# Two transformer blocks on one Trainium2 core: first MLP layer in two-tile units with merged matmuls, and a new order of small work at two norms

## The reference, cut to what matters

```python
        x = x + g1 * (mixed @ w_out[l])
        h2 = rms_norm(x) * (1.0 + sc2) + sh2
        x = x + g2 * (jnp.square(jax.nn.relu(h2 @ w_ff1[l])) @ w_ff2[l])
    return rms_norm(x, final_norm_w)
```

## Time and profile before

| what | value |
|---|---|
| time, median of 3 executions | 947.14 us (946.02 to 947.41) |
| the profiled execution | 945.35 us |
| its span, first to last instruction | 943.6 us |
| mean granted clock of PE | 0.989 of full |
| PE busy | 929.3 us, 98% |
| DVE busy | 708.4 us, 75% |
| ACT busy | 544.4 us, 58% |
| POOL busy | 118.6 us, 13% |
| moved by DMA | 175.47 MB, mean 186 GB/s |
| ff1 on PE | 428.2 to 520.8 us of the span |
| ff2 on PE | 520.8 to 610.6 us |
| in2's first group on PE | 610.6 to 626.7 us |

### The profile page before, as it was taken

How to read it: one execution, slowest core, us unless ns; L and a number is a source line. 1 busy time by engine, 2 the same in 40 slices (tenths; PEclk the granted TensorE clock), 3 DMA queues, 4 the chain that set the end, 5 groups by cost and what they waited for, 6 DMA issues and landing times.

```text
span 943.6 us, 17987 instructions
## 1 busy us (share of the span) xinstructions
PE 929.3 (98%) x6932; PEld 864.8 (92%) x6932; DVE 708.4 (75%) x934; ACT 544.4 (58%) x746; POOL 118.6 (13%) x95
## 2 busy tenths in 40 slices
PE   8999999999999999999999999999999999999997
PEld 5799999999899889989999888899878999999886
DVE  5947788889999968567666546679976698877664
ACT  4366655666676665455555435557675676666542
POOL 0000200035655400010000001302200100000000
PEclk8999999999999999999999999999999999999999
DMA  9954555577767756544566665535333356655661
GB/s 334 355 186 134 169 189 180 180 227 242 229 216 246 242 177 217 183 156 136 178 180 187 202 187 185 156 131 169 126 130 112 113 178 187 195 183 189 191 213 49
DMA packets 74952, 175.47 MB, mean 186 GB/s; under 512 B 5440, under 2 KB 32464, under 8 KB 74896
## 3 DMA queue, kind: packets, MB, share of 16 engines
q1 hardware_dynamic: 73920, 172.39, 56.5%
q0 software_dynamic: 368, 1.31, 0.4%
q10 hardware_dynamic: 608, 1.00, 0.3%
HBM read 173.63 MB, written 1.05 MB: 185 GB/s over the span
## 4 chain that ended last, share of the span: by engine, by line
PE 83%; DVE 11%; issue 3%; DMA 2%; ACT 1%; DVEq 0%; SPq 0%; ACTq 0%
PE proj_ps L1601 18%; PE proj_ps L1602 17%; PE proj_ps L1603 17%; PE proj_ps L1618 11%; PE proj_ps L1621 6%; DVE w_lo L925 4%; DVE mod_acc L937 3%; PE proj_ps L1661 1%; PE proj_ps L1662 1%; PE proj_ps L1663 1%; PE aux L1970 1%; PE aux L1689 1%; DMA mod_first<-in_panels 1%; PE aux L1697 1%; PE aux L1997 1%
## 5 line engine op out<-in xcount | busy, mean ns | idle before, releaser
L925 DVE TENSOR_TENSOR w_lo<-raw,w_hi 128x1024 fp32r<-128x1024 f32 x276 | 350.3, 1287 | 148.1 <-ACT w_hi L468 147.6
L468 ACT CAST w_hi<-raw 128x1024 fp32r<-128x1024 f32 x276 | 286.6, 1047 | 217.3 <-PE proj_ps L1603 101.5
L1601 PE MATMUL proj_ps<-act_pair,w_hi 128*128 128x256 f32 x1248 | 356.0, 285 | 0.0
L1603 PE MATMUL proj_ps<-act_pair,w_lo 128*128 128x256 f32 x1248 | 353.0, 283 | 0.0
L1602 PE MATMUL proj_ps<-act_pair,w_hi 128*128 128x256 f32 x1248 | 353.0, 283 | 0.0
L1601 PEld LDWEIGHTS proj_ps<-act_pair,w_hi 128*128 128x128 f32 x1248 | 239.2, 192 | 4.0 <-issue 2.5
L1602 PEld LDWEIGHTS proj_ps<-act_pair,w_hi 128*128 128x128 f32 x1248 | 239.3, 192 | 0.9 <-issue 0.2
L1603 PEld LDWEIGHTS proj_ps<-act_pair,w_lo 128*128 128x128 f32 x1248 | 239.3, 192 | 0.0
L1618 PE MATMUL proj_ps<-ff_pair,w_hi 128*128 128x512 f32 x256 | 69.9, 394 | 0.0
L432 POOL TENSOR_TENSOR tmp_b<-tmp_b 128x512 f32<-128x512 f32 x4 | 5.2, 1295 | 467.2 <-ACT tmp_b L491 467.2
L1618 PE MATMUL proj_ps<-glu_pair,w_hi 128*128 128x512 f32 x176 | 50.0, 395 | 0.0
(11 more groups left out here) (333 smaller groups left out, 1528.7 us busy)
## 6 DMA issues: line engine op xcount, KB each, us to landing
raw<-in_panels SPq DMA_DIRECT2D x308, 512.0 KB, 4.3
mod_first<-in_panels SPq DMA_DIRECT2D x16, 512.0 KB, 11.1
xres<-in_x_t SPq DMA_DIRECT2D x2, 512.0 KB, 6.3
out_t<-tmp_a SPq DMA_DIRECT2D x4, 256.0 KB, 2.1
wst<-in_ws_t POOLq DMA_DIRECT2D x1, 512.0 KB, 3.9
bs_sb<-in_bs_rows POOLq DMA_DIRECT2D x1, 512.0 KB, 4.9
level_sb<-in_levels ACTq DMA_DIRECT2D x1, 512.0 KB, 4.6
cols<-in_cols SPq DMA_DIRECT2D x1, 267.0 KB, 2.9
```

The source lines that it names most:

```text
L468: nc.scalar.copy(w_hi[:, s, :], raw[:, s, :]).then_inc(hi_done, 1)
L925: tt(out=w_lo[:, s, :], in0=raw[:, s, :], in1=w_hi[:, s, :].bitcast(F32), op=ALU.subtract).then_inc(taken, 1)
L1601: mm(dst, hi, xh, start=first and k == 0 and nt % 2 == 0, stop=False, skip_group_check=True)
L1603: ins = mm(dst, lo, xh, start=False, stop=last and k == ks - 1, skip_group_check=True)
```

## The change

ff1's group 1 stays a chunk, now in half 1 of `proj_ps`. Groups 2 to 8 become 14 units of two tiles, two slots each, run by `unit_panel` and loaded by `load_unit`. Since a bank now holds two halves, ACT copies the second half of a unit's two banks to `half_sb`, DVE adds the first half to it (`ffsum_sb`), and takes max(s, 0) * s in one operation (`ffsq_sb`), which is relu and square; ACT copies the high part and DVE subtracts for the low part. PE's wait for a free half becomes a wait for the square. The loops of ff1 are written out. At the norm in front of ff1 the residuals of tiles 6 and 7 go ahead of `split_lo` of slots 0 and 1, and `split_lo` of slot 2 moves into the norm, behind tile 3. In in2 the column sums come one tile at a time behind the first three half panels, and `row_of` behind the fifth.

```diff
-EVAC_XBC, EVAC_ZG, EVAC_FF1, EVAC_IN2, EVAC_UP = 4, 12, 20, 27, 33
+EVAC_XBC, EVAC_ZG, EVAC_FF1, EVAC_IN2, EVAC_UP = 4, 12, 20, 34, 40
...
-            with sp.Fori(out_rg + 2, ff2) as i:
+            for s in range(SLOTS):
+                load(out_rg + 2, s)
+            for rg in range(out_rg + 3, ff2):
                 for s in range(SLOTS):
-                    load(i, s)
+                    load_unit(rg, s, rg, s // 2, s % 2)
...
-            for s in range(2):
-                split_hi(GROUP["ff1"], s)
+            split_hi(GROUP["ff1"], 0)
             squares((6,), RES_OUT)
+            split_hi(GROUP["ff1"], 1)
             split_hi(GROUP["ff1"], 2)
             squares((7,), RES_OUT)
...
+            split_all(GROUP["ff1"] + 1)
+            evac(relu_sb[:, 0].rearrange("p (n t) -> p n t", n=NT), GROUP["ff1"], 1, ACT.Relu)
+            act.wait_ge(S["sq_ok"], 1)
+            nc.scalar.copy(ff_hi[:, 0:NT], sq_sb[:, 0].rearrange("p (n t) -> p n t", n=NT)).then_inc(S["ffhi_ok"], 1)
+
+            def small_half(u):
+
+                act.wait_ge(used, (GROUP["ff1"] + 1) * SLOTS + 2 * u + 2)
+                nc.scalar.copy(half_sb[:, u % 2], proj_ps[:, u % 2].rearrange("p (n a t) -> p n a t", n=2, a=2)[:, :, 1]
+                               ).then_inc(evac_act, 1)
+
+            def ff_high(u):
+                act.wait_ge(S["sq_ok"], u + 2)
+                nc.scalar.copy(ff_hi[:, 2 * u + 4:2 * u + 6], ffsq_sb[:, u % 2]).then_inc(S["ffhi_ok"], 1)
+
+            for c in range(1, 8):
+                for h in range(2):
+                    split_hi(GROUP["ff1"] + c + 1, 2 * h)
+                    small_half(2 * c - 2 + h)
+                    split_hi(GROUP["ff1"] + c + 1, 2 * h + 1)
+                    ff_high(2 * c - 2 + h)
...
             add_unit(1, (4, 5), 16)
-            split_lo(GROUP["ff1"], 0)
             dve.wait_ge(S["bank_done"], 1)
             add_unit(0, (6,), 16)
-            split_lo(GROUP["ff1"], 1)
+            split_lo(GROUP["ff1"], 0)
             dve.wait_ge(used, (GROUP["out"] + 2) * SLOTS)
             add_unit(0, (7,), 16)
-            split_lo(GROUP["ff1"], 2)
+            split_lo(GROUP["ff1"], 1)
...
+            norm_apply(1, lambda k: modc[:, 32 + k:33 + k], lambda k: modc[:, 24 + k:25 + k],
+                       lambda k: split_lo(GROUP["ff1"], {3: 2, 7: 3}[k]) if k in (3, 7) else None)
...
+            def ff_square(u):
+
+                dve.wait_ge(evac_act, EVAC_FF1 + u + 2)
+                step(tt(out=ffsum_sb[:, u % 2], in0=half_sb[:, u % 2],
+                        in1=proj_ps[:, u % 2].rearrange("p (n a t) -> p n a t", n=2, a=2)[:, :, 0], op=ALU.add))
+                stt(out=ffsq_sb[:, u % 2], in0=ffsum_sb[:, u % 2], scalar=0.0, in1=ffsum_sb[:, u % 2], op0=ALU.max,
+                    op1=ALU.mult).then_inc(S["sq_ok"], 1)
...
+            def ff_low(u):
+                dve.wait_ge(S["ffhi_ok"], u + 2)
...
+            for c in range(1, 8):
+                for h in range(2):
+                    split_lo(GROUP["ff1"] + c + 1, 2 * h)
+                    ff_square(2 * c - 2 + h)
+                    split_lo(GROUP["ff1"] + c + 1, 2 * h + 1)
+                    ff_low(2 * c - 2 + h)
...
+            chunk(GROUP["ff1"], 1, x_ready=(S["nrm_lo"], KT))
+            for u in range(14):
+                if u == 1:
+                    pe.wait_ge(evac_act, EVAC_FF1 + 1)
+                elif u > 1:
+                    pe.wait_ge(S["sq_ok"], u)
+                for kk in range(2):
+                    unit_panel(GROUP["ff1"] + 1 + u // 2, 2 * (u % 2) + kk, u % 2, act_hi, act_pair, kk, 4, kk == 0)
             for u in range(4):
                 if u < 2:
-                    pe.wait_ge(evac_act, EVAC_FF1 + 7 + u)
+                    pe.wait_ge(S["sq_ok"], 14 + u)
...
-                    pe.wait_ge(S["ff_ok"], 2 * (kk // 2) + 2)
+                    pe.wait_ge(S["ff_ok"], 4 * (kk // 2) + 3)
...
             def beside_in2(s, half):
+                if (s, half) == (0, 0):
+                    mean_square(2, (0,), True)
                 if (s, half) == (0, 1):
-                    mean_square(2, (0, 6, 7), True)
-                if (s, half) == (1, 1):
+                    mean_square(2, (6,), True)
+                if (s, half) == (1, 0):
+                    mean_square(2, (7,), True)
+                if (s, half) == (2, 0):
                     row_of(2)
```

More of the change, by code:

```diff
@@ L160, in two_blocks @@
         ff_hi, ff_lo = ff_pair[:, :, 0], ff_pair[:, :, 1]
-        relu_sb = at("relu_sb", 136, [2, NT * T])
-        sq_sb = at("sq_sb", 144, [2, NT * T])
+        relu_sb = at("relu_sb", 136, [1, NT * T])
+        sq_sb = at("sq_sb", 144, [1, NT * T])
+        half_sb = at("half_sb", 148, [2, 2, T])
+        ffsum_sb = at("ffsum_sb", 152, [2, 2, T])
+        ffsq_sb = at("ffsq_sb", 156, [2, 2, T])
         q_sb = at("q_sb", 72, [4, T])
@@ L1265, in _ @@
             broadcast(1, stat[:, 1])
[L1266 to L1275, removed]
@@ L1277, in _ @@
-            with dve.Fori(0, 4) as i:
-                ff1_step(i * 2, 0)
-                ff1_step(i * 2 + 1, 1)
+            norm_apply(1, lambda k: modc[:, 32 + k:33 + k], lambda k: modc[:, 24 + k:25 + k],
+                       lambda k: split_lo(GROUP["ff1"], {3: 2, 7: 3}[k]) if k in (3, 7) else None)
+            split_all(GROUP["ff1"] + 1)
+            dve.wait_ge(evac_act, EVAC_FF1 + 1)
+            tt(out=sq_sb[:, 0], in0=relu_sb[:, 0], in1=relu_sb[:, 0], op=ALU.mult).then_inc(S["sq_ok"], 1)
@@ new lines, in _ @@
+            dve.wait_ge(S["ffhi_ok"], 1)
+            tt(out=ff_lo[:, 0:NT], in0=sq_sb[:, 0].rearrange("p (n t) -> p n t", n=NT), in1=ff_hi[:, 0:NT].bitcast(F32),
+               op=ALU.subtract).then_inc(S["ff_ok"], 1)
+            def ff_square(u):
[4 more added lines that the diff above has]
+                    op1=ALU.mult).then_inc(S["sq_ok"], 1)
@@ new lines, in ff_low @@
+            def ff_low(u):
+                dve.wait_ge(S["ffhi_ok"], u + 2)
+                part = slice(2 * u + 4, 2 * u + 6)
+                tt(out=ff_lo[:, part], in0=ffsq_sb[:, u % 2], in1=ff_hi[:, part].bitcast(F32), op=ALU.subtract).then_inc(S["ff_ok"], 1)
+            for c in range(1, 8):
[4 more added lines that the diff above has]
+                    ff_low(2 * c - 2 + h)
```

## The result

| | before | after |
|---|---|---|
| median of 4 executions each, us | 947.12 (946.02 to 947.41) | 939.51 (938.80 to 941.84) |
| ratio, 95% interval | | 0.9926 (0.9907 to 0.9945) |
| the profiled execution, us | 945.35 | 941.84 |
| its span, us | 943.6 | 940.1 |
| mean granted clock | 0.989 | 0.993 |

7.6 us faster, 5.2 to 8.8 by the interval. The direction was right, the size was not.

A forecast was written before the change was run, and what follows sets the result against it. PE was taken as the bound, busy for 98% of the span. Gains of 2.06 + 1.1 + 0.4 = 3.6 us gave 943.5 us against the median of 947.14, chance 0.50, range 941.0 to 946.3.

The forecast's parts named there:

- Part 1: ff1: two-tile units with merged matmuls bring 28 slots from 2.880 to 2.807 us each, gaining 2.06 us on PE.
- rival C: ff1: DVE becomes the bound, at ff_square behind w_lo; at most 6 us slower, about 950 us; chance 0.07.
- Rival D: ff1: merging matmuls saves nothing, the 2.06 us falls away and 1.5 is left, 945.6 us; chance 0.03.
- Part 2: Norm before ff1: residuals ahead of w_lo start sum, root, row_of and norm earlier; 1.1 us taken, ends 0 and 1.8.
- case for the clock that stays up: Norm before ff1: without the low clock row_of is short and the chunk starts near 426.5; gain 1.8 us.
- the case of 0.5: Norm before ff1: the low clock comes at the same moment again, keep_clock ends near 427.6; gain 0.5 us.
- Part 3: in2: column sums over three half panels avoid the low clock; 0.4 us taken, ends -0.5 and 1.3.
- What PE is ahead by more than some 0.4 it waits away there: Behind in2's norm: DVE and POOL bound, so of PE's 0.8 us lead only 0.4 us is kept.
- Rival A: ff1's norm and in2: the clock stays up at both, gaining 5.2 us, 941.9 us; chance 0.21.
- Rival B: ff1's norm and in2: the low clock comes back, leaving a gain of 1.6 us, 945.5 us; chance 0.19.
- 1 us of scatter: Whole kernel: allowance on the fast side of the range, setting its low end at 941.0 us.

The follow-up runs named there:

- sums_only: Kernel before with only in2's column sums in three parts and row_of later; median 945.04 us, ratio 0.9994 to the kernel before.
- units_only: Kernel before with only ff1's two-tile units, old order at the norm and old column sums; median 945.02 us, ratio 0.9991 to the kernel before.
- slot2_front: Kernel after with the w_lo of slot 2 back in front of the norm; norm 7.03 us against 6.37, whole kernel 939.38 us.
- units_norm: Kernel after with in2's column sums as before; median 941.74 us, ratio 0.9964 to the kernel before.
- level_late: Kernel after with one unused DVE add of 128x256 ahead of the first level's difference; levels took 39.65 us against 39.47.
- norm_only: Kernel before with only the new order of residuals and w parts at ff1's norm; median 945.06 us, ratio 0.9997 to the kernel before.
- all_three: Kernel after, unchanged, run again beside the single parts; median 940.24 us, ratio 0.9950 to the kernel before.
- all_again: Kernel after, unchanged, run once more beside the pairs of parts; median 941.58 us, ratio 0.9958 to the kernel before.
- norm_sums: Kernel after without ff1's units, with both new orders; median 943.15 us, ratio 0.9978 to the kernel before.

## Why the prediction was wrong in size

The forecast was 3.6 us and the medians gave 7.6. Of the 4.0 us between them, 1.05 lie at the norm (2.15 in place of 1.1) and 1.12 in in2 (1.52 in place of 0.4), both terms of the sum that were too small; the other 1.9 lie in none of the three places.

**Part 1 was right to 0.01 us.** 28 slots were to give 2.06; ff1 gives 92.04 - 89.98 = 2.06, and 89.97 or 89.98 us stand in all ten kernels with units. The 64 half slots of ff2 were the right row. The rule of the Trainium skill that spoke against it (TensorE: Matmul & The Clock Gate, section Back-to-back issue gap) would have given 0.6. The section gives it for an isolated matmul and says that in a stream the weight loads set the spacing too, and the trace agrees that it doesn't price a merge in this kernel: 9 ns each in place of 2.5. Each merge also takes away one weight load (PEld x6932 before, x6708 after, 224 fewer); which of the two gives the 9 ns no run separates. What stands beside PE held as well. The groups of after, 445 to 515 us:

```profile
L940 DVE TENSOR_TENSOR w_lo<-raw,w_hi 128x1024 fp32r<-128x1024 f32 x25 | 30.5, 1221 | 2.0 <-ACT w_hi L473 2.0
...
L1295 DVE SCALAR_TENSOR_TENSOR ffsq_sb<-ffsum_sb 128x512 f32<-128x512 f32 x13 | 9.0, 692 | 0.4
L1293 DVE TENSOR_TENSOR ffsum_sb<-half_sb,proj_ps 128x512 f32<-128x512 f32 x13 | 8.9, 687 | 12.3 <-ACT half_sb L731 12.3
...
L731 ACT COPY half_sb<-proj_ps 128x512 f32<-128x512 f32 x13 | 7.6, 587 | 20.1 <-PE proj_ps L1651 20.0
```

687, 692 and 587 ns stand where 688, 688 and 590 were taken from the earlier trace rows. ACT waits for PE, DVE for ACT, and PE for none of them: rival C is refuted, with room for two more operations a unit. Rival D is refuted too.

**Part 2 was right as a mechanism; the value taken was the wrong case, and that case was set too small.** The chain of after at the norm:

```profile
423.35 1.30 PE aux L1706 x12
424.68 0.27 ACT stat L517
...
425.72 0.70 PE aux L1714 x2
426.42 1.72 PE aux L1675 x4
428.14 0.36 issue
428.50 0.35 PE proj_ps L1631
```

and the timeline of DVE there, where residual 7 stands directly behind PE's last tile:

```profile
422.53 1.00 DVE L1044 SCALAR_TENSOR_TENSOR xres<-proj_ps,modc,xres 128x256 f32<-128x256 f32 x2 [0.67 <-PE proj_ps L1651]
```

At an unbroken clock the order is worth 1.10 us, as forecast (1.1). With the low clock gone too, it was 2.15: 1.10 for the order, 0.87 for the clock, and the 0.18 that go with the units. I had a case for the clock that stays up, at 1.8, and took 1.1, between it and the case of 0.5 in which the low clock comes again. sums_only shows that the low clock isn't bound to the old order: there it stayed away without the new one. The other three profiled executions with the old order had it (before, units_only, units_sums); of the ten with residual 7 going first (slot2_front among them) none.

**Part 3 failed as a term.** 0.4 us was taken, 1.52 came in the profiled pair. The step that failed is "What PE is ahead by more than some 0.4 it waits away there". The chain of after in in2:

```profile
610.08 0.79 PE aux L1706 x8
...
612.41 0.79 PE aux L1706 x8
...
614.74 0.79 PE aux L1706 x8
...
618.50 0.43 PE aux L1714 x2
```

There are three errors in it. The first is PE's lead, 0.8 us in the prediction and 1.52 in the trace: units_norm, with the old sums and the clock up, takes 14.61 us in in2, so the low clock cost 16.12 - 14.61 = 1.51 and not 1.3, and three groups of sums (14.60) cost no more than one, where 0.5 was set for the two more changes between kinds. The second is the norm's first product on DVE: it came 11.24 us after in2's first matmul, against 11.33 before, and not 0.4 later. The third is the chain behind it. That DVE is busy for 10.00 of 10 us was read in the levels; between the norm and the first level DVE and ACT waited, in before, for PE or for each other:

```profile
633.56 0.88 DVE L1340 TENSOR_SCALAR og<-aux,cols 128x256 f32<-128x256 f32 x2 [0.40 <-PE aux L1943]
637.06 0.38 ACT L503 COPY r_sb<-aux 128x256 f32<-128x256 f32 x1 [1.23 <-PE aux L1684]
642.31 0.69 DVE L1005 SCALAR_TENSOR_TENSOR gt<-gt,og 128x512 f32<-128x512 f32 x1 [0.69 <-ACT og L775]
```

With PE ahead, DVE's two waits are gone and ACT's is 0.29, so the chain moved forward with PE: the first level's difference came 33.85 us after in2's first matmul, against 35.21. The product on POOL ended before PE wanted it, which is here to be read:

```profile
649.20 0.86 POOL L458 TENSOR_TENSOR gx<-gqk,gd 128x256 f32<-128x256 f32 x1
```

```profile
650.27 1.16 PE L2007 MATMUL aux<-gx 64*128 64x128 f32 x16
```

650.06 against 650.27, a cover of 0.21 us, where before had 0.39. level_late shows the same 0.2 from the other side. PE was 1.52 us ahead and waited nothing away; the prediction had it wait from 0.4 on. Yet the 1.52 takes no work away: T x c is the same with and without the new sums, and units_norm has the old ones at 14.61. They are worth 1.5 us beside an execution whose clock falls there, nothing beside one whose clock doesn't, and over the sets 1.3 in the clock's column. With the old sums it fell in two of four profiled executions (before, norm_only), with the new ones in none of ten. Whether order and sums make a fall rarer, and not merely move it, these counts suggest and don't settle.

**Rival A came nearest** for a profiled pair: 2.06 + 2.15 + 1.52 = 5.73 against its 5.2. In the repeated sets the change gives 5.3 and 4.1 us by the medians, one near that and one nearer to the forecast's 3.6. Rival B named what does happen (a clock that moves between executions) and got its place wrong. Its rule, of the Trainium skill (TensorE: Matmul & The Clock Gate, section What's actually happening), that the moment of the gate is free-running against the kernel, agrees with these runs: after, all_three and all_again are one kernel, and the clock was low near 46 us in the first and the third and near 262 in the second and the third.

**The range failed on the scatter.** It gave "1 us of scatter". The same unchanged start takes 416.1 to 421.0 us, and the kernel before spans 943.0 to 948.6 in 64 executions. Of the first pair's 7.6 us, 4.1 to 5.3 come back in the repeated sets. Before's first median, 947.12, is 1.5 over its medians of 29 and 35 executions, and after's, 939.51, is 0.7 and 2.1 under those of all_three and all_again. That the latter is the luck of four executions (their low clock took 5.9 us, against 5.5 and 7.3 in the sets) is the likeliest reading and not shown apart.

**What stays open:** what brings the low clock at out in the second block. It was there in six of the fourteen profiled executions. That it comes because the clock was not low in in2 does not fit norm_only, where it was low at both places, nor all_three, after, norm_sums and four more, where it was low at neither; no run was made to tell. The single parts' medians hang on this: units_only's missing 2 us are lost to the low clock, but why just that kernel loses most is not known.

## What to carry to other kernels

Where PE has no hole, price a merge of matmuls by the distance of starts in a stage that already has the new shape; it held here to 0.01 us in 92. Before a wait is said to eat a gain, measure its cover from both sides: when the late operand is ready and when it is taken, both counted from the stage's first matmul, and after the change as well. Where the granted clock dips in unchanged code, split each kernel's mean time into T x c and T x (1 - c) before comparing; medians of one kernel, from 4 and from 12 executions, differ here by 2 us with no difference in the code. Such a split is an estimate, and T x (1 - c) scatters by more than the parts are worth.

## What the runs showed of the hardware

- Low stretches of the clock recur at a few places, in some executions only: of the 14 profiled ones near 45 us in 11, near 262 in 6, at ff1's norm in 3, in in2 in 2, at out of the second block in 6, and once at 334 (sums_only). At the norm one cost 0.9 us, in in2 1.5, at out 1.6; all together, those at the kernel's start and end included, make 5.5 to 10.9 us of 945 by T x (1 - c).
- A DVE record of 128x1024 lasts 1.22 us, and the next operation starts 1.14 behind it; for 128x512, 0.69 and 0.60. Two operations more a unit put DVE at 68.52 of 70 us, and PE waited for none of it.
- 24 records of one column take 2.58 us in units_norm, at a clock of 1.00, and 2.82 in before, where the clock fell during the last of them. In one run or in three times eight, they make no difference to in2 (14.61 and 14.60 us) at an unbroken clock.
- One matmul of 512 columns in place of two of 256 saves 0.0733 us a slot, 28 slots 2.06 us; eight merges are in a slot, so 9 ns each, with one weight load less for each, and the other eight matmuls are as before.
